# Unnormalized queries and keys in the gated delta rule of a hybrid block: the query scale in the output norm, the key scales in the rows of the triangular system

## The chip, the cores and the metric

One NeuronCore of a Trainium2 chip runs the whole block; nothing is shared with other cores. The time is the device time of one execution in microseconds. It was taken three times for the kernel before, and once more with the hardware profiler. TensorE multiplies matrices, VectorE, ScalarE and GpSimd work on tiles, and SyncE issues most loads.

## The reference, cut to what matters

The block reads 512 rows of width 2048 and sums three branches. The change is in the first one, a gated delta rule with 8 heads of width 128:

```python
qkv = jax.nn.silu(causal_depthwise_conv(qkv_raw, conv_w))
q = l2norm(q) * (GDN_HEAD_DIM ** -0.5)      # l2norm(x) = x * rsqrt(sum(x * x) + EPS)
k = l2norm(k)
k_beta = k * beta[..., None]
lower = where(strict, einsum(k_beta, k) * decay, 0)
rhs = concatenate([v * beta, k_beta * exp(gc)])
sol = triangular_solve(eye + lower, rhs)    # u_val, w_dec
qk = einsum(q, k) * decay
...                                         # scan over chunks: v_new, o, state
o = rmsnorm(o, out_norm_g)                  # o * rsqrt(mean(o * o) + EPS) * g
```

`beta` is a sigmoid per row and head, `gc` a running sum of log decays, `decay` their exponentiated differences. The other branches are a diagonal state space layer (S5) and an attention to 256 memory rows; gates, a projection and a last norm follow.

## The kernel before, in words

The program has five phases: attention, a mixer phase for the delta rule and S5 (with the projections of x for them), the gated unit of S5, the three merges, and the output projection. Nearly all of TensorE's work is the projections. A weight block of 128 output columns (16 tiles of 128x128) is loaded by SyncE into `raw`, split by ScalarE into a high part (`split_hi`, L406) and by VectorE into a low part (`split_lo`, L413), and multiplied with the high and low part of the activations: three products of 512 columns per tile (`mm3`, L419 to L421). `raw`, `wh` and `wl` have two buffers each. ScalarE copies the finished block out of its PSUM bank (`tile_out`).

**The mixer phase is a pipeline of three stages, written out by hand for each engine.** In one round, stage a runs the six projection blocks of head i, stage j the first part of head i-1 (convolution, norms, the triangular system and its inverse by levels, S5), and stage l the second part of head i-2 (weights, new values, states, output, output norm). Rounds for heads 0, 7 and the last output are unrolled; the six in between are a loop whose semaphore targets lie in registers. Each engine has a function `mixer` whose lines are the order of its queue. TensorE's (L924 to L991) places one piece of j or l work between eighths of a block, each of six products.

The order around the change, per round:

- TensorE: `norm_keys` (L789: the sum of squared keys over the partitions, L793, and running sums of decays, L796) behind the sixth eighth of block 1; `norm_queries` (L798) behind the second eighth of block 2; then `keys` (transposes of `kc`, L812), `keys_keys` (L820), `values` (L806), `turn_lower` (transposes of `dl`, L835), `keys_queries` (L828), and the levels, of which `level_x` 1 (L847) is the first. `level_x` 1 waits for `du`, which VectorE writes at L1651. `output_norm` (L894) is the sum of squared outputs.
- ScalarE (L1291 to L1313): `activation_of` (silu and the squares of queries and keys, L1240 and L1243), a sine table for S5, `output_root`, `key_root` (L1245: the root of the key sums, then `er`, an exponential), a sine table (L1227 to L1230), the copy-out of block 1 (`kraw`), L406 for block 3, `query_root` (L1252), `decays` (exponentials of `du` and `dl`, L1259 and L1261), and so on. Square roots, exponentials and sines each need a table load, which the compiler inserts.
- VectorE (L1720 to L1741): `convolve` for queries, keys and values, L413, four S5 combinations and scans, `gated` (L1683: a reciprocal and two products, the last being L1690), `differences` (L1606), `normed_keys` (a 128x512 reciprocal, L1619, and a product, L1621), L413 for block 3, `normed_queries` (L1625, L1627), `keys` (L1640, L1641), `system` (L1646), `values` (L1631), S5 combinations, `first_level` (L1657 to L1663), `queries` (L1651), L413, `level_x` 1.
- GpSimd (L552 to L620): arguments of the sines (`farg`), `turn_back` for S5, the store of the head before, `masks` (three products over 128x512, L594, L597 and L599, behind `decays`), further arguments, `decayed_queries` (L604), `turn_back`. VectorE's `keys` waits for the third of the masks (`pm` 3), `system` for the second.

`hph` holds four values per row and chunk of one head: `beta` (0), the sum of decays (1), `beta` times its exponential (2), and the log decay (3). PSUM bank 2 holds the squared-query sums, then the turned values, then keys by queries; bank 6 the squared-key sums, the turned keys and the turned `dl`; bank 7 the decays, then keys by keys.

The waits that tie `keys` to the others:

```python
dve.wait_ge(k.ktr, count(j, 1, 1))      # keys turned, TensorE
dve.wait_ge(k.dec, count(j, 2, 2))      # decays, ScalarE
dve.wait_ge(k.pm, count(j, 3, 4))       # third mask, GpSimd
tt(k.kbg[:, :, :], chunked(ps[6][:, :]), rows(k.hph[:, 2, :]), ALU.mult)
```

Of the kernel before, what the change touches and what calls it, by code (L numbers as in the profile page):

```python
# [51 lines left out]
COLS = ["eps", "eps128", "quarter", "even", "odd", "neven", "nodd"]  # L52
# [9 lines left out]
def constants():  # L62
# [11 lines left out]
    for n, v in enumerate([EPS, P * EPS, np.pi / 2, g2 == 0, g2 == 1, -(g2 == 0).astype(float), -(g2 == 1).astype(float)]):  # L74
        c[:, C_COL + n] = v
# [34 lines left out]
def build(nc, x, mem, norm_g, w_in, conv_w, a_log, dt_bias, gdn_g, lam_re, lam_im, log_dt, b_re, b_im,  # L110
          c_re, c_im, s5_d, w_glu, mem_g, w_kv, w_a, w_b, w_c, w_out, final_g, consts, out):
    with ExitStack() as ctx:
# [71 lines left out]
        with ExitStack() as area:  # L184
# [110 lines left out]
        k.qk, k.vtr, k.vb_s, k.ktr, k.kb, k.kk = \  # L295
            sems("qk", "vtr", "vb_s", "ktr", "kb", "kk")
# [236 lines left out]
def pool_program(k, pool):  # L533
# [18 lines left out]
    def mixer(j, l):  # L552
# [132 lines left out]
def tensor_program(k, pe):  # L685
# [238 lines left out]
    def mixer(a, j, l):  # L924
# [161 lines left out]
def scalar_program(k, act):  # L1086
# [150 lines left out]
    def activation_of(j, n):  # L1237
        t, sq = ((k.qc, k.rq), (k.kc, k.rk), (k.vc, None))[n]
        act.wait_ge(k.conv, count(j, 4 * n + 4, 12))
        act.activation(t[:, :], t[:, :], ACT.Silu).then_inc(k.silu, 1)  # L1240
        if sq is not None:
            act.wait_ge(k.silu, count(j, n + 1, 3))
            act.activation(sq[:, :], t[:, :], ACT.Square).then_inc(k.sq, 1)  # L1243

    def key_root(j):  # L1245
# [45 lines left out]
    def mixer(a, j, l, gate=None):  # L1291
# [580 lines left out]
```

## Time and profile before

| | |
|---|---|
| median of three runs | 2503.39 us (2502.95 to 2505.22) |
| span of the profiled execution | 2498.6 us |
| time of the profiled execution outside its span | not given on its own; the median lies 4.8 us above the span |
| TensorE busy | 2334.3 us, 93% |
| VectorE busy | 1211.7 us, 48% |
| ScalarE busy | 734.8 us, 29% |
| GpSimd busy | 696.0 us, 28% |
| mixer phase | about 441 to 1620 us, most heads some 130 us apart |

The profile's timelines list instructions by engine with their start and length; an instruction that stood idle before it has the idle time and the engine and line that ended it in brackets. Operations on one engine overlap by some hundredths of a microsecond. The granted clock is TensorE's, as a share of 2.4 GHz: 1.00 is 2.4 GHz and 0.50 is 1.2 GHz. L numbers are lines of the kernel before.

### The profile page before, as it was taken

The numbers are of one execution on the slowest core, as the hardware profiler recorded it, in microseconds if no ns is written. First come the engines' busy times: TensorE is split into PE (matmuls) and PEld (weight loads), VectorE is DVE, ScalarE is ACT, GpSimd is POOL, SyncE is SP. The second block draws the span as 40 slices with busy tenths as digits, with TensorE's granted clock in tenths as the row PEclk, the third lists the DMA queues.
The fourth block names the chain that finished last, engine by engine and source line by source line (L and its number), as shares of the span: only waits on it lengthen the run. The fifth ranks groups of instructions, "written<-read, shape, count | busy, mean of one in ns | idle before, by whom it ended". The sixth has DMA issues, their size and how long they took to land.

```text
span 2498.6 us, 28934 instructions
## 1 busy us (share of the span) xinstructions
PE 2334.3 (93%) x10744; PEld 1841.5 (74%) x10744; DVE 1211.7 (48%) x1319; ACT 734.8 (29%) x831; POOL 696.0 (28%) x538
## 2 busy tenths in 40 slices
PE   4999989999999999999989899989999999999996
PEld 3888868676666666666767578878888888887885
DVE  4433322858676776767685842333322232334223
ACT  5433322414142424232333423321221221223221
POOL 0000000756656565758483820010000000000000
PEclk9999999899999999998989899999999999999998
DMA  4544423222121122222222135544533333333332
GB/s 163 137 118 124 121 84 94 67 55 62 51 65 48 50 52 59 57 59 57 59 57 63 51 85 152 158 150 140 166 101 99 87 100 102 89 96 118 118 131 88
DMA packets 367431, 232.96 MB, mean 93 GB/s; under 512 B 20538, under 2 KB 348419, under 8 KB 365827
## 3 DMA queue, kind: packets, MB, share of 16 engines
q1 hardware_dynamic: 355954, 193.21, 28.6%
q0 software_dynamic: 9104, 34.61, 3.9%
q10 hardware_dynamic: 2304, 4.20, 0.4%
q8 instruction: 48, 0.79, 0.1%
q14 instruction: 21, 0.16, 0.0%
HBM read 213.11 MB, written 18.87 MB: 93 GB/s over the span
## 4 chain that ended last, share of the span: by engine, by line
PE 72%; POOL 11%; DVE 6%; issue 4%; ACT 4%; DMA 1%; POOLq 0%; SPq 0%; DVEq 0%; ACTq 0%
PE bank L419 21%; PE bank L421 21%; PE bank L420 21%; POOL karg L571 2%; PE bank L847 1%; POOL farg L573 1%; PE bank L857 1%; POOL karg L567 1%; POOL farg L569 1%; ACT wh L406 1%; PE bank L856 1%; DVE wl L413 1%; POOL pt L585 1%; POOL dl L594 1%; POOL hr L587 1%
## 5 line engine op out<-in xcount | busy, mean ns | idle before, releaser
L413 DVE TENSOR_TENSOR wl<-raw,wh 128x2048 fp32r<-128x2048 f32 x176 | 413.9, 2352 | 729.9 <-ACT wh L406 729.9
L419 PE MATMUL bank<-uh,wh 128*128 128x512 f32 (+1 forms) x1808 | 757.1, 419 | 4.9 <-POOLq L362 4.6
L420 PE MATMUL bank<-ul,wh 128*128 128x512 f32 (+1 forms) x1808 | 715.9, 396 | 0.0
L421 PE MATMUL bank<-uh,wl 128*128 128x512 f32 x1792 | 711.4, 397 | 0.0
L406 ACT ACTIVATE wh<-raw 128x2048 fp32r<-128x2048 f32 x176 | 336.1, 1910 | 429.2 <-PE bank L421 399.7
L419 PEld LDWEIGHTS bank<-uh,wh 128*128 128x128 f32 (+1 forms) x1808 | 346.1, 191 | 135.3 <-issue 66.8
L421 PEld LDWEIGHTS bank<-uh,wl 128*128 128x128 f32 x1792 | 343.8, 192 | 77.2
L420 PEld LDWEIGHTS bank<-ul,wh 128*128 128x128 f32 (+1 forms) x1808 | 346.8, 192 | 72.8 <-issue 8.1
L419 PE MATMUL bank<-gh,wh 128*128 128x512 f32 x512 | 202.6, 396 | 8.3 <-DVE gl L1779 8.3
L421 PE MATMUL bank<-gh,wl 128*128 128x512 f32 x512 | 201.0, 393 | 0.0
L420 PE MATMUL bank<-gl,wh 128*128 128x512 f32 x512 | 200.3, 391 | 0.0
L672 POOL DMA_DIRECT2D fg<-in_final_g_dram x1 | 0.6, 558 | 520.2 <-DVEq L362 520.2
L419 PEld LDWEIGHTS bank<-gh,wh 128*128 128x128 f32 x512 | 96.8, 189 | 28.9 <-issue 8.7
L421 PEld LDWEIGHTS bank<-gh,wl 128*128 128x128 f32 x512 | 96.6, 189 | 22.5
L420 PEld LDWEIGHTS bank<-gl,wh 128*128 128x128 f32 x512 | 96.7, 189 | 21.0
L541 POOL DMA_DIRECT2D gated_c<-ox x8 | 4.5, 563 | 365.6 <-DVE ox L1480 365.1
L419 PE MATMUL bank<-wh,uh 128*128 128x512 f32 x256 | 100.2, 391 | 3.3 <-DVE ul L1829 3.3
L421 PE MATMUL bank<-wh,ul 128*128 128x512 f32 x256 | 100.3, 392 | 0.0
L420 PE MATMUL bank<-wl,uh 128*128 128x512 f32 x256 | 100.3, 392 | 0.0
L1382 ACT ACTIVATE gates<-bank 128x512 f32<-128x512 f32 x32 | 19.1, 598 | 273.1 <-PE bank L421 273.1
L847 PE MATMUL bank<-tl,lt 128*128 128x128 f32 x384 | 58.9, 303 | 41.4 <-DVE du L1651 39.8
L847 PEld LDWEIGHTS bank<-tl,lt 128*128 128x128 f32 x384 | 55.4, 213 | 50.0 <-issue 42.9
(308 smaller groups left out, 3218.7 us busy)
## 6 DMA issues: line engine op xcount, KB each, us to landing
raw<-in_w_in_dram SPq DMA_DIRECT2D x224, 512.0 KB, 4.9
raw<-in_w_kv_mem_dram SPq DMA_DIRECT2D x32, 512.0 KB, 5.1
raw<-in_w_out_dram SPq DMA_DIRECT2D x32, 512.0 KB, 4.4
raw<-in_s_w_glu_dram SPq DMA_DIRECT2D x16, 512.0 KB, 5.1
raw<-in_w_br_c_dram SPq DMA_DIRECT2D x16, 512.0 KB, 5.0
raw<-in_w_br_b_dram SPq DMA_DIRECT2D x16, 512.0 KB, 4.7
raw<-in_w_br_a_dram SPq DMA_DIRECT2D x16, 512.0 KB, 4.6
xs<-in_x_dram SPq DMA_DIRECT2D x4, 1024.0 KB, 8.4
```

Source lines behind the costliest of these rows:

```text
L406: act.activation(k.wh[slot][:, :], k.raw[slot][:, :], ACT.Copy).then_inc(k.w_hi, 1)
L413: dve.tensor_tensor(k.wl[slot][:, :], k.raw[slot][:, :], k.wh[slot][:, :].bitcast(F32), ALU.subtract).then_inc(k.w_lo, 1)
L419: pe.matmul(o, ah, bh, start=start, stop=False)
L420: pe.matmul(o, ah, bl, start=False, stop=False)
L421: return pe.matmul(o, al, bh, start=False, stop=stop)
L567: ts(k.karg[:, :], k.karg[:, :], -ROUND, None, ALU.add).then_inc(k.args, 1)
L569: tt(k.farg[:, :], k.farg[:, :], k.karg[:, :], ALU.subtract).then_inc(k.args, 1)
L571: ts(k.karg[:, :], k.tvec, lo_, None, ALU.mult).then_inc(k.args, 1)
L573: tt(k.farg[:, :], k.farg[:, :], k.karg[:, :], ALU.add).then_inc(k.args, 1)
L585: pool.tensor_tensor(k.pt[:, :], c2[:, :], b[:, :], ALU.mult).then_inc(k.dem, 1)
L587: pool.tensor_tensor(o[:, :], o[:, :], k.pt[:, :], op).then_inc(k.dem, 1)
L847: mm = pe.matmul(ps[2][:, n * P:(n + 1) * P], k.lt[:, n, :], k.tl[:, n, :], start=True, stop=True)
```

## The change

The keys and queries are no longer divided by their norms. With s the inverse of the squared key norm of a row (plus epsilon), the triangular system becomes one for scaled unknowns: its row factor is `beta` times s instead of `beta`, `kbg` takes s as well, and the values take `beta` times the root of s. The sum of squared keys is taken with the rows on partitions, four narrow products into a 128x4 piece of bank 6, and VectorE works on 128x4 pieces (`hk`) where it worked on 128x512. The query norm is left to the output norm: the squared queries, times epsilon and constants, are added to the squared outputs in one PSUM group.

- Removed: `norm_queries` (TensorE), `query_root` (ScalarE), `normed_keys` and `normed_queries` (VectorE), the semaphore `qk`.
- Added: `key_scales` (VectorE, four 128x4 operations, in front of `differences`), one 128x4 product in `values`, a second product in `output_norm`, a 128x4 root in `key_root`.
- Moved: the squares (`key_squares` before the values' silu, `query_squares` behind `output_root`); `key_root` behind `row_decays` (the exponential `er`); it waits for `rn` 2, VectorE's reciprocal.
- New waits: GpSimd's second mask for `rn` 4, TensorE's `keys` for `rn` 1, VectorE's `convolve` for `sq` of the head before.

```diff
 # GpSimd, masks and decayed_queries
             wait_apart(k, pool, k.pm, count(j, 1, 4))
+            wait_apart(k, pool, k.rn, count(j, 4, 4))
             pool.tensor_tensor(k.dl[:, :, :], k.dl[:, :, :],
-                               k.hph[:, 0, :].unsqueeze(2).to_broadcast([P, NT, P]), ALU.mult).then_inc(k.pm, 1)
+                               k.hk[:, 2, :].unsqueeze(2).to_broadcast([P, NT, P]), ALU.mult).then_inc(k.pm, 1)
...
-            wait_apart(k, pool, k.qk, count(j, 2, 2))
+            wait_apart(k, pool, k.silu, count(j, 1, 3))
+            wait_apart(k, pool, k.er_s, count(j, 1, 1))
 # TensorE
-        pe.wait_ge(k.sq, count(j, 2, 2))
+        pe.wait_ge(k.sq, count(j, 1, 2))
         wait(pe, k.oroot, count(j, 0, 1))
-        pe.matmul(ps[6][:, :], ones, k.rk[:, :], start=True, stop=True).then_inc(k.ss, 1)
+        for n in range(NT):
+            mm = pe.matmul(ps[6][:, n:n + 1], k.rk[:, n * P:(n + 1) * P], ones[:, 0:1], start=True, stop=True)
+        mm.then_inc(k.ss, 1)
...
-    def norm_queries(j):
-        wait(pe, k.og, count(j, 0, 2))
-        pe.matmul(ps[2][:, :], ones, k.rq[:, :], start=True, stop=True).then_inc(k.ss, 1)
     def values(j):
         pe.wait_ge(k.silu, count(j, 3, 3))
-        pe.wait_ge(k.root, count(j, 2, 2))
+        wait(pe, k.og, count(j, 0, 2))
...
     def keys(j):
-        pe.wait_ge(k.qk, count(j, 1, 2))
+        pe.wait_ge(k.silu, count(j, 2, 3))
+        pe.wait_ge(k.rn, count(j, 1, 4))
...
     def keys_queries(j):
-        pe.wait_ge(k.qk, count(j, 2, 2))
+        pe.wait_ge(k.silu, count(j, 1, 3))
...
     def output_norm(j):
         pe.wait_ge(k.osq, count(j, 1, 1))
-        pe.matmul(ps[6][:, :], ones, k.lt[:, :, :], start=True, stop=True).then_inc(k.sso, 1)
+        pe.wait_ge(k.sq, count(j, 2, 2))
+        pe.matmul(ps[6][:, :], ones, k.lt[:, :, :], start=True, stop=False)
+        pe.matmul(ps[6][:, :], ones, k.rq[:, :], start=False, stop=True).then_inc(k.sso, 1)
 # ScalarE
+    def key_squares(j):
+        act.wait_ge(k.silu, count(j, 2, 3))
+        wait(act, k.ss, count(j, 0, 1))
+        act.activation(k.rk[:, :], k.kc[:, :], ACT.Square).then_inc(k.sq, 1)
+    def query_squares(j):
+        act.wait_ge(k.silu, count(j, 1, 3))
+        wait(act, k.sso, count(j, 0, 1))
+        act.activation(k.rq[:, :], k.qc[:, :], ACT.Square, scale=P * EPS ** 0.5).then_inc(k.sq, 1)
...
     def key_root(j):
-        act.wait_ge(k.ss, count(j, 1, 2))
-        act.activation(k.rk[:, :], ps[6][:, :], ACT.Sqrt, bias=col["eps"]).then_inc(k.root, 1)
+        act.wait_ge(k.rn, count(j, 2, 4))
+        act.activation(k.hk[:, 3, :], k.hk[:, 0, :], ACT.Sqrt).then_inc(k.root, 1)
...
-        if j: s5_matrices(j); activation_of(j, 1); activation_of(j, 2); s5_tables(j, 0)
+        if j: s5_matrices(j); activation_of(j, 1); key_squares(j); activation_of(j, 2); s5_tables(j, 0)
         if l: output_root(l)
-        if j: key_root(j); s5_tables(j, 1)
+        if j: query_squares(j); row_decays(j); key_root(j); s5_tables(j, 1)
         if a: out(1); split(2)
-        if j: query_root(j); decays(j); keep_z(j)
+        if j: decays(j); keep_z(j)
 # VectorE
+    def key_scales(j):
+        dve.wait_ge(k.ss, count(j, 1, 1))
+        ts(k.hk[:, 0, :], ps[6][:, 0:NT], EPS, None, ALU.add).then_inc(k.rn, 1)
+        dve.wait_ge(k.rn, count(j, 1, 4))
+        dve.reciprocal(k.hk[:, 0, :], k.hk[:, 0, :]).then_inc(k.rn, 1)
+        dve.wait_ge(k.rn, count(j, 2, 4))
+        tt(k.hk[:, 1, :], k.hk[:, 0, :], k.hph[:, 2, :], ALU.mult).then_inc(k.rn, 1)
+        tt(k.hk[:, 2, :], k.hk[:, 0, :], k.hph[:, 0, :], ALU.mult).then_inc(k.rn, 1)
     def values(j):
+        dve.wait_ge(k.root, count(j, 1, 1))
+        tt(k.hk[:, 3, :], k.hk[:, 3, :], k.hph[:, 0, :], ALU.mult).then_inc(k.kscale, 1)
         dve.wait_ge(k.vtr, count(j, 1, 1))
-        tt(k.vb[:, :, :], chunked(ps[2][:, :]), rows(k.hph[:, 0, :]), ALU.mult).then_inc(k.vb_s, 1)
+        dve.wait_ge(k.kscale, count(j, 1, 1))
+        tt(k.vb[:, :, :], chunked(ps[2][:, :]), rows(k.hk[:, 3, :]), ALU.mult).then_inc(k.vb_s, 1)
...
         wait(dve, k.vtr, count(j, 0, 1))
+        wait(dve, k.sq, count(j, 0, 2))
...
-        if j: differences(j); normed_keys(j)
+        if j: key_scales(j); differences(j)
         if a: split(2)
-        if j: normed_queries(j); keys(j); system(j); values(j); s5_states(j, 1, 0); s5_states(j, 1, 1)
+        if j: keys(j); system(j); values(j); s5_states(j, 1, 0); s5_states(j, 1, 1)
```

## Rows read from the trace of the kernel before

**Rows 1.** The page, section 2: TensorE's busy tenths in 40 equal slices of the span.

```profile
PE   4999989999999999999989899989999999999996
```

**Rows 2.** The windows of one head: start:end, length, busy us (instructions) of TensorE matmuls, weight loads, VectorE, ScalarE, GpSimd; granted clock; DMA share; GB/s.

```profile
981.50:1111.50 130.00, 118.49 (x538) 86.89 (x538) 92.33 (x108) 41.48 (x52) 83.17 (x60) 0.93 0.21 56
```

**Rows 3.** TensorE's timeline: start, us, engine, line, operation, count, in brackets idle before.

```profile
892.72 1.98 PE L847 MATMUL bank<-tl,lt 128*128 128x128 f32 x8 [5.00 <-DVE du L1651]
...
982.31 1.10 PE L793 MATMUL bank<-rk,cst 128*128 128x512 f32 x2 [0.91 <-ACT lt L1288]
983.24 1.02 PE L796 MATMUL bank<-gx,cst 128*128 128x512 f32 x2
...
993.49 2.07 PE L800 MATMUL bank<-rq,cst 128*128 128x512 f32 x2 [3.75 <-DVE kbg L1690]
...
1022.47 2.02 PE L847 MATMUL bank<-tl,lt 128*128 128x128 f32 x8 [4.97 <-DVE du L1651]
```

**Rows 4.** VectorE's timeline in the same head.

```profile
992.40 1.03 DVE L1690 TENSOR_TENSOR kbg<-kbg,zk 128x512 f32<-128x512 f32 x1
...
996.23 3.34 DVE L1619 RECIPROCAL rk<-rk 128x512 f32<-128x512 f32 x1
999.60 0.69 DVE L1621 TENSOR_TENSOR kc<-kc,rk 128x512 f32<-128x512 f32 x1
1000.21 2.28 DVE L413 TENSOR_TENSOR wl<-raw,wh 128x2048 fp32r<-128x2048 f32 x1
1002.41 3.35 DVE L1625 RECIPROCAL rq<-rq 128x512 f32<-128x512 f32 x1
1005.79 0.82 DVE L1627 TENSOR_TENSOR qc<-qc,rq 128x512 f32<-128x512 f32 x1
1006.54 0.68 DVE L1640 TENSOR_TENSOR kbg<-bank,hph 128x512 f32<-128x512 f32 x1
...
1021.64 0.68 DVE L1651 TENSOR_TENSOR du<-bank,du 128x512 f32<-128x512 f32 x1
```

**Rows 5.** ScalarE's timeline in the same head.

```profile
990.60 1.28 ACT L1227 ACT_TABLE_LOAD   x1 [4.56 <-POOL farg L575]
...
996.10 1.28 ACT L1255 ACT_TABLE_LOAD   x1
...
998.10 1.28 ACT L1259 ACT_TABLE_LOAD   x1
...
999.93 0.61 ACT L1261 ACTIVATE dl<-dl 128x512 f32<-128x512 f32 x1
```

**Rows 6.** GpSimd's timeline in the same head.

```profile
1000.73 2.88 POOL L594 TENSOR_TENSOR dl<-dl,cst 128x512 f32<-128x512 f32 x1 [0.38 <-ACT dl L1261]
...
1004.79 1.28 POOL L599 TENSOR_TENSOR du<-du,cst 128x512 f32<-128x512 f32 x1
```

**Rows 7.** Single lines of the program: count, then nanoseconds minimum/median/maximum, first and last start.

```profile
L594 POOL TENSOR_TENSOR dl<-dl,cst x8: 1268/2880/2888, 483.4 to 1390.9; 128x512 f32<-128x512 f32 x8
...
L1405 ACT ACTIVATE stat<-stat,cst x1: 298/298/298, 2480.9 to 2480.9; 128x4 f32<-128x4 f32 x1
...
L1432 DVE RECIPROCAL stat<-stat x2: 165/172/178, 22.6 to 28.2; 128x4 f32<-128x4 f32 x1, 128x2 f32<-128x2 f32 x1
```

**Rows 8.** Timelines of heads 0 (VectorE) and 7 (GpSimd), which stand outside the loop.

```profile
487.44 0.69 DVE L1640 TENSOR_TENSOR kbg<-bank,hph 128x512 f32<-128x512 f32 x1 [2.27 <-POOL du L599]
...
503.69 0.68 DVE L1651 TENSOR_TENSOR du<-bank,du 128x512 f32<-128x512 f32 x1
...
1390.90 2.39 POOL L594 TENSOR_TENSOR dl<-dl,cst 128x512 f32<-128x512 f32 x1 [1.50 <-ACT dl L1261]
```

**Rows 9.** Windows around the clock's return in two heads, and head 7's restart.

```profile
1032.00:1033.00 1.00, 1.00 (x4) 0.77 (x4) 0.00 (x0) 0.00 (x0) 1.00 (x2) 0.63 0.00 0
...
1413.14 2.05 PE L847 MATMUL bank<-tl,lt 128*128 128x128 f32 x8 [6.00 <-DVE du L1651]
...
1421.50:1422.00 0.50, 0.50 (x3) 0.40 (x2) 0.00 (x0) 0.00 (x0) 0.50 (x2) 0.64 0.00 0
```

More of the change, by code:

```diff
@@ L51 @@
 C_COL = C_T + S
-COLS = ["eps", "eps128", "quarter", "even", "odd", "neven", "nodd"]
+COLS = ["eps", "epssq", "quarter", "even", "odd", "neven", "nodd"]
 NCONST = C_COL + len(COLS)
@@ L73, in constants @@
     g2 = np.arange(P) // GS % 2
-    for n, v in enumerate([EPS, P * EPS, np.pi / 2, g2 == 0, g2 == 1, -(g2 == 0).astype(float), -(g2 == 1).astype(float)]):
+    for n, v in enumerate([EPS, P * EPS * EPS, np.pi / 2, g2 == 0, g2 == 1, -(g2 == 0).astype(float), -(g2 == 1).astype(float)]):
         c[:, C_COL + n] = v
@@ L209, in build @@
             k.hph = sb(area, "hph", [4, NT])
+            k.hk = sb(area, "hk", [4, NT])
             k.s5h = sb(area, "s5h", [5, 4])
@@ L294, in build @@
             sems("rsum", "root", "er_s", "dd", "dec", "rn")
-        k.qk, k.vtr, k.vb_s, k.ktr, k.kb, k.kk = \
-            sems("qk", "vtr", "vb_s", "ktr", "kb", "kk")
+        k.kscale, k.vtr, k.vb_s, k.ktr, k.kb, k.kk = \
+            sems("kscale", "vtr", "vb_s", "ktr", "kb", "kk")
         k.kq, k.pm, k.lm, k.qkt, k.ltr, k.lt_s = \
@@ L953, in mixer @@
         if a: big(a, 1, 6, 7); big(a, 2, 0, 1)
-        if j: norm_queries(j)
         if a: big(a, 2, 2, 3)
@@ L1237, in activation_of, with row_decays, key_root @@
     def activation_of(j, n):
-        t, sq = ((k.qc, k.rq), (k.kc, k.rk), (k.vc, None))[n]
+        t = (k.qc, k.kc, k.vc)[n]
         act.wait_ge(k.conv, count(j, 4 * n + 4, 12))
         act.activation(t[:, :], t[:, :], ACT.Silu).then_inc(k.silu, 1)
[L1241 to L1245, printed above, removed]
-        act.wait_ge(k.ss, count(j, 1, 2))
-        act.activation(k.rk[:, :], ps[6][:, :], ACT.Sqrt, bias=col["eps"]).then_inc(k.root, 1)
+    def key_squares(j):
[6 more added lines that the diff above has]
+        act.activation(k.rq[:, :], k.qc[:, :], ACT.Square, scale=P * EPS ** 0.5).then_inc(k.sq, 1)
+    def row_decays(j):
         act.wait_ge(k.rsum, count(j, 1, 1))
         act.activation(k.er[:, :, :], ps[7][:, :].rearrange("p (n c) -> p n c", n=NT), ACT.Exp).then_inc(k.er_s, 1)
-    def query_root(j):
-        act.wait_ge(k.ss, count(j, 2, 2))
-        act.activation(k.rq[:, :], ps[2][:, :], ACT.Sqrt, bias=col["eps128"], scale=float(P)).then_inc(k.root, 1)
+    def key_root(j):
+        act.wait_ge(k.rn, count(j, 2, 4))
+        act.activation(k.hk[:, 3, :], k.hk[:, 0, :], ACT.Sqrt).then_inc(k.root, 1)
     def decays(j):
@@ L1287, in output_root @@
         act.wait_ge(k.sso, count(l, 1, 1))
-        act.activation(k.lt[:, :, :], ps[6][:, :].rearrange("p (n c) -> p n c", n=NT), ACT.Sqrt, bias=col["eps"],
+        act.activation(k.lt[:, :, :], ps[6][:, :].rearrange("p (n c) -> p n c", n=NT), ACT.Sqrt, bias=col["epssq"],
                        scale=1 / P).then_inc(k.oroot, 1)
@@ L1615, in differences @@
         ts(k.dl[:, :, :], k.dl[:, :, :], 0.0, None, ALU.max).then_inc(k.dd, 1)
-    def normed_keys(j):
-        dve.wait_ge(k.root, count(j, 1, 2))
-        dve.reciprocal(k.rk[:, :], k.rk[:, :]).then_inc(k.rn, 1)
-        dve.wait_ge(k.rn, count(j, 1, 2))
-        tt(k.kc[:, :], k.kc[:, :], k.rk[:, :], ALU.mult).then_inc(k.qk, 1)
-    def normed_queries(j):
-        dve.wait_ge(k.root, count(j, 2, 2))
-        dve.reciprocal(k.rq[:, :], k.rq[:, :]).then_inc(k.rn, 1)
-        dve.wait_ge(k.rn, count(j, 2, 2))
-        tt(k.qc[:, :], k.qc[:, :], k.rq[:, :], ALU.mult).then_inc(k.qk, 1)
+    def key_scales(j):
[6 more added lines that the diff above has]
+        tt(k.hk[:, 2, :], k.hk[:, 0, :], k.hph[:, 0, :], ALU.mult).then_inc(k.rn, 1)
     def values(j):
+        dve.wait_ge(k.root, count(j, 1, 1))
+        tt(k.hk[:, 3, :], k.hk[:, 3, :], k.hph[:, 0, :], ALU.mult).then_inc(k.kscale, 1)
         dve.wait_ge(k.vtr, count(j, 1, 1))
-        tt(k.vb[:, :, :], chunked(ps[2][:, :]), rows(k.hph[:, 0, :]), ALU.mult).then_inc(k.vb_s, 1)
+        dve.wait_ge(k.kscale, count(j, 1, 1))
+        tt(k.vb[:, :, :], chunked(ps[2][:, :]), rows(k.hk[:, 3, :]), ALU.mult).then_inc(k.vb_s, 1)
     def keys(j):
@@ L1639, in keys @@
         wait(dve, k.g_st, count(j, 0, 16))
-        tt(k.kbg[:, :, :], chunked(ps[6][:, :]), rows(k.hph[:, 2, :]), ALU.mult).then_inc(k.kb, 1)
+        dve.wait_ge(k.rn, count(j, 3, 4))
+        tt(k.kbg[:, :, :], chunked(ps[6][:, :]), rows(k.hk[:, 1, :]), ALU.mult).then_inc(k.kb, 1)
         tt(k.kd[:, :, :], chunked(ps[6][:, :]), k.du[:, :, P - 1:P].to_broadcast([P, NT, P]), ALU.mult).then_inc(k.kb, 1)
```

## Prediction

> **What bounds the kernel now.** I read the page first. TensorE's slices are nearly all nines [rows 1], so a change pays only where TensorE waits or runs at its lower clock. Then the windows cut per head: in the mixer stage TensorE is busy 118.5 of 130 us and its mean granted clock is 0.93 [rows 2]; a head takes 129.7 us, from the restart at L847 at 892.72 to the next at 1022.47 [rows 3]. So about 11.5 us of a head are idle and some 9 us of clock (0.07 x 130) are lost. Its timeline says where: 4.97 us before L847 on VectorE's `du` (L1651), 3.75 us before L800 on `kbg` (L1690), 0.91 us before L793 on ScalarE's `lt` [rows 3]. The change touches the first two.
>
> Which of them sets a head's end? After the wait at L800, TensorE runs some 24 us of work and then stops again at L847 until 1022.47 [rows 3]. Whatever it gains before 1017.5 it waits away at L847. So L847's release decides, and that is VectorE's L1651. VectorE is busy without a gap from 980.5 to 1022.3; the stretch from L1690 to L1651 is shown in [rows 4]. At first sight 8 us leave just this chain. So I followed the two engines that feed it: ScalarE, whose `dl` exponential (L1261) ends at 1000.54 [rows 5], and GpSimd, whose masks start 0.2 us later and end at 1006.07 [rows 6]. VectorE's `keys` (L1640) waits for the third mask and starts at 1006.54. So the GpSimd chain is only 0.47 us short of being the bound today.
>
> **The change part by part, in the head that starts at 981.5.**
>
> VectorE loses L1619 (3.34 us), L1621 (0.69), L1625 (3.35) and L1627 (0.82): 8.2 us [rows 4]. It gains five operations of 128x4; one costs about 0.2 us with its wait, by the 128x4 reciprocal of 178 ns [rows 7]. Four of them stand behind `gated`, so `differences` ends near 997 and VectorE then waits for the split of block 3 (L413, behind ScalarE's L406).
>
> ScalarE loses `query_root` (a table load and the root, from 996.10 to the next load at 998.10 [rows 5]) from in front of the exponentials: 2.0 us. The two squares stay, moved; the query one stands behind `output_root`, where ScalarE next waits for TensorE or GpSimd. But `key_root` now needs `rn` 2, two small VectorE operations behind L1690, and that ends at 992.40 + 1.03 = 993.43 [rows 4]. Small operations 0.4 and 0.1 of signalling give 993.9. Then a load of 1.28 and a 128x4 root of 0.30 [rows 7] end at 995.5. Everything ScalarE did from the load at 990.60 to the one at 996.10 (sine table, `kraw`, L406) stands behind it: 5.5 us, to 1001.0. The exponential table, `du` and `dl` took 998.10 to 1000.54, 2.44 us: they end at 1003.5, that is **2.9 us later** than before. What is queued behind the new wait is thus all of ScalarE's work up to L1261, and GpSimd waits for that. The loads of the loop start only after the wait in front of them: the one at 990.60 came after 4.56 us of idling [rows 5], so I don't let the root's load hide. The second sine table, `kraw` and block 3's high half come 4.9 us later too, and L413 behind it frees `raw` for SP's next load 0.9 us later; their users on VectorE and TensorE stand behind 1008, and SP's load of about 5 us has until ScalarE's next L406 at 1013, so I put these at nothing.
>
> GpSimd starts L594 at 1003.6 instead of 1000.73. It took 2.88 us there, since it began while VectorE's L413 ran (1000.21 to 1002.49); the fastest of the eight took 1.27 [rows 4, 6, 7]. Now L413 runs from 1001.05 to 1003.35, just ahead of it, and VectorE then idles: I take 1.27. That returns 1.6 us, and the third mask is done 1.3 us later, at 1007.4. `keys` starts 0.1 behind it: 1007.5 against 1006.54, +0.95. The scale in `values` adds 0.2 and the extra waits of `convolve` 0.05. L1651 and with it L847 come **1.2 us later**. L594 at its old 2.88 is the upper end for this step (+2.8); full cover by the 0.47 us of today and no signalling is the lower one (+0.8).
>
> TensorE: `norm_queries` goes (two passes of 512 columns, 0.93 us by L793's at full clock [rows 3]), and its wait; eight narrow products replace L793's two, bounded between nothing and 1.9, twice what L793 takes; I take the same 0.93. New waits at `keys` (`rn` 1, 993.6), `keys_keys` and, above all, `turn_lower`: it needs L1646, now near 1009, while TensorE arrives near 1004.5. None of this counts, for TensorE still reaches L847 before 1020, even with 5 us at the lower clock; the cover is the wait at L847, which grows to 5 us or more. `output_norm` gains one product, 0.93 us. In a head it fits the 0.9 us before L793 [rows 3], where otherwise it would cost 0.9. In the last round there is no such wait: it is paid once.
>
> VectorE from L1640 to L1651 took 15.1 us with GpSimd working beside it [rows 4]; in head 0 the same stretch took 16.3 (487.44 to 503.69 [rows 8]). How the two engines meet changes a little, so between -1 and +1.1 us a head; I take nothing, as the two start as far apart as before (2.7 against 2.8 us).
>
> The lower clock: it comes back 10.3 us after the restart at 1022.47 (the row from 1032 is low for 0.74 us), but 8.7 us after the one at 1413.14 [rows 3, 9]. A us at 1.2 GHz instead of 2.4 costs half a us of work: 4.4 to 5.1 us a head. New restarts will fall elsewhere in this span; I take back 0.3 a head, bounds -0.8 and +0.8.
>
> Six heads in the loop: 6 x (1.2 - 0.3) = 5.4. Head 0 has no `gated`, and its `keys` already waited 2.27 us for the mask [rows 8], which waits for GpSimd's own queue: +0.2. Head 7's loads are 1.28 us for each gate output too; there L594 took 2.39 [rows 8] and gives back only 1.1 of 2.9, less the cover of 0.4, plus the scale: +1.6. Last round +0.9. **Sum +8.1 us.** The profiled span of 2498.6 becomes 2506.7; the median of the runs lies 4.8 above that span, and gives 2511.5.
>
> A page speaks against more: the Trainium skill, "ScalarE: Activation LUTs", section "What ACT_TABLE_LOAD costs", puts a drain of 1.38 us behind each load, 2.66 us in all. By that the three loads behind `rn` 2 would make L1651 4.1 us later still, and the kernel some 33 us slower than my sum; the rows show 1.28 us and a function 0.01 us behind it (998.10 + 1.28, `dl` done by 1000.54) [rows 5], so this rival has a chance below 0.01.
>
> **The rivals.**
> (a) The delay is returned by the clock, or GpSimd has less to wait: L1651 comes 0.8 us later or less, and the clock, coming back at an unchanged moment after a later restart, gives most of it back. Then only the last round and head 7 remain: +2 to +3, about 2506. For it: head 7's late restart lost less [rows 9]. Chance 0.3.
> (b) Faster: ScalarE's root isn't held by `gated`. The place is `key_root`'s wait; the point is whether `rn` 2 is there before GpSimd has computed `farg` (990.4). Then `dl` ends 2 us earlier, L594 starts unblocked near 1000.7 and takes 1.27, and `keys` starts near 1004.6: -1.9 + 0.2, some -1.7 us for seven heads, with the last round about -11: 2492. Against it: two VectorE operations and 3.3 us of reciprocal stand in front of `rn` 2 in program order. Chance 0.12.
> (c) L594 still collides with L413 (the margin is 0.3 us), or the stretch to L1651 takes head 0's 16.3 us: 1.1 to 1.6 us more in six heads, 2518 to 2521. Chance 0.12.
> (d) The saved VectorE time reaches L847 whole (8 heads x 7 us, 2447): it would need `keys` to start near 1000, before GpSimd has masks to give. 0.01.
> My forecast has 0.45, and its far lower tail (VectorE and GpSimd meeting better by 1 us a head) reaches below 2498 with 0.01.
>
> **How the numbers follow.** 0.2% is 5 us, about what a measurement of this kernel can tell. Forecast and (c) are slower by more, and a tenth of (a) too; the forecast's lower tail falls within 5 us. Slower 0.55, same 0.31, faster 0.14. The range from 2498 to 2518 leaves out (b), (d) and half of (c), 0.19 in all.
>
> **What the new profile would show.** `key_root`'s load starting near 994 after a wait for VectorE; L1261 ending near 1003.5 on this head's clock; L594 at 1.3 us; VectorE idle near 997 to 1001 and 1003.3 to 1007.5, the second on GpSimd's `du`; TensorE waiting about 5 us before the transposes of `dl` and over 5 before the first level; none before the keys but 1 to 2 us; a head of about 130.6 us. Wrong if `keys` isn't waiting for GpSimd, if the exponentials end before 1001, or if a head is under 129.7 us.

## The result, and the profile after

The changed kernel took **2522.98 us** in the median of 4 runs (2521.75 to 2524.17), the kernel before 2504.3 in 4 runs beside it (2502.95 to 2505.92): a ratio of 1.0078, 95% interval 1.0064 to 1.0092. It is slower by 19 us. The forecast was 2511.5, slower, with a range to 2518: the direction was right, the size less than half of what came, and the time is outside the range. The profiled execution has a span of 2520.6 us, 22.0 above the one before: TensorE's idle time grew by 13.6 us (164.3 to 177.9) and its busy time by 8.4.

The page of the changed kernel, busy time and the slices of TensorE and its clock:

```profile
PE 2342.7 (93%) x10792; PEld 1848.0 (73%) x10792; DVE 1169.3 (46%) x1327; ACT 723.5 (29%) x822; POOL 679.1 (27%) x538
...
PE   4999989899898989898989799999999999999996
...
PEclk9999999999898989898979899999999999999998
```

VectorE's four instructions did go (its busy time falls from 1211.7 to 1169.3 us), yet TensorE's slices show more eights in the mixer stage than [rows 1]. Who makes TensorE wait there? The waits of the changed kernel's TensorE from 441 to 1650 us (engine, tile and line, releaser; us in total, times, longest):

```profile
PE bank L849 <- DVE du L1663: 68.6, 8, 9.7
PE bank L814 <- DVE hk L1630: 7.8, 7, 1.5
PE bank L822 <- DVE dl L1622: 7.6, 7, 1.1
```

and the same of the kernel before, from 441 to 1620 us:

```profile
PE bank L847 <- DVE du L1651: 39.8, 8, 6.0
PE bank L800 <- DVE kbg L1690: 25.7, 7, 3.8
PE bank L812 <- DVE kc L1621: 8.7, 8, 4.0
```

The 34 us of waits for `kbg` and `kc` have become 15, and the wait for `du` has grown from 39.8 to 68.6. So the new time is in VectorE's chain to `du`. The head that answers to [rows 4 to 6] has its `gated` at 1003.61, where the old one had 992.40. ScalarE's timeline in it:

```profile
996.05 1.28 ACT L1264 ACT_TABLE_LOAD   x1
1005.00 0.20 ACT L1264 ACTIVATE hk<-hk 128x4 f32<-128x4 f32 x1 [7.67 <-DVE hk L1632]
1005.22 1.28 ACT L1230 ACT_TABLE_LOAD   x1
...
1012.55 0.61 ACT L1270 ACTIVATE dl<-dl 128x512 f32<-128x512 f32 x1
```

VectorE and GpSimd in the same head, in one timeline (L1702 is the old L1690, L595 the old L594, L1652 the old L1640, L1721 the old L1709, L570 the old L569, L1725 the old L1713, L1669 the old L1657, L1663 the old L1651). Two instructions in it matter most: `gr`, VectorE's product for the S5 scans, and `farg`, GpSimd's product for the arguments of the sines; both have two inputs in SBUF:

```profile
1003.61 1.08 DVE L1702 TENSOR_TENSOR kbg<-kbg,zk 128x512 f32<-128x512 f32 x1
...
1010.74 2.29 DVE L414 TENSOR_TENSOR wl<-raw,wh 128x2048 fp32r<-128x2048 f32 x1 [1.79 <-ACT wh L407]
...
1013.36 1.28 POOL L595 TENSOR_TENSOR dl<-dl,cst 128x512 f32<-128x512 f32 x1 [1.79 <-ACT dl L1270]
...
1017.20 0.69 DVE L1652 TENSOR_TENSOR kbg<-bank,hk 128x512 f32<-128x512 f32 x1 [4.17 <-POOL du L601]
...
1019.01 0.15 DVE L1639 TENSOR_TENSOR hk<-hk,hph 128x4 f32<-128x4 f32 x1
1019.26 0.69 DVE L1642 TENSOR_TENSOR vb<-bank,hk 128x512 f32<-128x512 f32 x1
...
1021.17 1.29 POOL L570 TENSOR_TENSOR farg<-farg,karg 128x512 f32<-128x512 f32 x1 [0.18 <-POOL karg L568]
1021.18 1.82 DVE L1721 TENSOR_TENSOR gr<-ma,mb 128x512 f32<-128x512 f32 x1
...
1025.09 2.19 DVE L1725 TENSOR_TENSOR_SCAN gr<-s5h,gr 128x512 f32<-128x512 f32 x1
1027.21 1.56 DVE L1725 TENSOR_TENSOR_SCAN gi<-s5h,gi 128x512 f32<-128x512 f32 x1
1028.69 1.69 DVE L1669 TENSOR_TENSOR tl<-dl,cst 128x512 f32<-128x512 f32 x1
...
1035.32 0.68 DVE L1663 TENSOR_TENSOR du<-bank,du 128x512 f32<-128x512 f32 x1
```

and the lines of the kernel before that stand between the L1640 and L1651 of [rows 4]:

```profile
1010.24 0.69 DVE L1709 TENSOR_TENSOR gr<-ma,mb 128x512 f32<-128x512 f32 x1
1010.39 1.71 POOL L569 TENSOR_TENSOR farg<-farg,karg 128x512 f32<-128x512 f32 x1 [0.18 <-POOL karg L567]
...
1013.02 1.59 DVE L1713 TENSOR_TENSOR_SCAN gr<-s5h,gr 128x512 f32<-128x512 f32 x1
1014.53 1.19 DVE L1713 TENSOR_TENSOR_SCAN gi<-s5h,gi 128x512 f32<-128x512 f32 x1
1015.65 1.71 DVE L1657 TENSOR_TENSOR tl<-dl,cst 128x512 f32<-128x512 f32 x1
```

Counted from the end of `gated` (993.43 before, 1004.69 after):

| from the end of `gated`, in the head read | before | after |
|---|---|---|
| `dl` exponential ends | 7.1 | 8.5 |
| third mask ends | 12.6 | 12.5 |
| `keys` starts | 13.1 | 12.5 |
| `keys` to the first level (L1657, L1669) | 9.1 | 11.5 |
| `keys` to `du` (L1651, L1663) | 15.1 | 18.1 |

`keys` starts 0.6 us earlier, yet `du` comes 2.4 later: the stretch from `keys` to `du` takes **3.0 us longer**. The timelines say where. The scale product puts `vb` 0.25 later (the pitch from `dl` to `vb` was 0.60 and is 0.85). The product `gr` started 0.15 us ahead of GpSimd's `farg` before and took 0.69, while `farg` took 1.71. Now it starts 0.01 us behind `farg` and takes 1.82, while `farg` takes 1.29: its pitch to the next instruction is 1.13 longer. The scans give up another 0.97 (2.63 from the first one to the first level before, 3.60 now), and the four products from there to `du` 0.64. Together 2.99.

A theory comes from that: two products of inputs in SBUF, one on each engine, don't run side by side, and the one that starts first goes through. (The pair at 1021.17 lasts 1.83 us from its first start to its last end, where 0.69 and 1.29 in turn would be 1.98.) The change moved the phase of the two queues by a hair. Against GpSimd's instruction behind the masks (1006.17, L564, before; 1017.27, L565, after) `keys` started 0.37 us late and now starts 0.07 early: VectorE gained 0.44. From `keys` to `gr` it is 3.70 us before and 3.98 after (the scale product): 0.28 lost. And GpSimd reaches `farg` 4.22 us behind that instruction before, 3.90 after: 0.32 lost. So a lead of 0.15 became a lag of 0.01. The rivals: the 3 us are the scale product and its waits themselves, or they come from the later exponentials.

### The profile page after: what moved, and what is told of

It reads as the page before. It is cut to its first block, busy times and chain, and to the rows that moved or that the text cites. A ratio compares the mean times of both kernels' runs of the same rounds, so it can differ in the third digit from the quotient of the medians.

```text
span 2520.6 us, 29089 instructions
## 1 busy us (share of the span) xinstructions
PE 2342.7 (93%) x10792; PEld 1848.0 (73%) x10792; DVE 1169.3 (46%) x1327; ACT 723.5 (29%) x822; POOL 679.1 (27%) x538
## 4 chain that ended last, share of the span: by engine, by line
PE 77%; DVE 11%; issue 4%; ACT 3%; POOL 2%; DMA 1%; DVEq 0%; SPq 0%; POOLq 0%; ACTq 0%
PE bank L420 22%; PE bank L422 22%; PE bank L421 21%; PE bank L849 2%; PE bank L859 2%; PE bank L858 1%; PE bank L918 1%; PE bank L925 1%; DVE gi L1725 1%; PE bank L926 1%; PE bank L919 1%; DVE tl L1697 1%; DVE mb L1719 1%; DVE gr L1721 1%; PE bank L754 1%
## 5 line engine op out<-in xcount | busy, mean ns | idle before, releaser
L849 PE MATMUL bank<-tl,lt 128*128 128x128 f32 x384 | 59.1, 303 | 68.6 <-DVE du L1663 68.6
```

What stands on the lines that cost most here:

```text
L849: mm = pe.matmul(ps[2][:, n * P:(n + 1) * P], k.lt[:, n, :], k.tl[:, n, :], start=True, stop=True)
```

## The experiments

Runs 1 to 4 stood beside a kernel before of 2502.47 us (23 runs), runs 5 to 8 beside 2501.92 (7 runs), run 9 beside 2501.7 (7 runs). Ratios are against these.

**1. The scale product in front of `keys`.** The same work, but done in VectorE's idle time.

```
+    def value_scale(j):                       # its wait and its product, out of values
...
-        if j: keys(j); system(j); values(j); ...
+        if j: value_scale(j); keys(j); system(j); values(j); ...
```

> The changed kernel with one line moved: VectorE makes the 128x4 scale of the values in front of keys, where it stands idle, and no longer between system and values. In the changed kernel the stretch from the start of kbg to the start of du takes 18.1 us a head against 15.1 before, and the first S5 difference gr in it starts 0.01 us behind GpSimd's farg product and takes 1.82 us instead of 0.69. Theory A (the two engines exclude each other, and who starts first decides): VectorE is now 0.25 us earlier and comes first, so the stretch falls by 2 to 3 us to 15 to 16, and the kernel to 2500 to 2509 us. Theory B (the stretch grew by the work and the waits put into it): it falls by the 0.25 us that left it, the kernel to about 2521.

2505.69 us (2503.31 to 2507.08, 10 runs), ratio 1.0013 [1.0003, 1.0022]: of the 18.7 us over the kernel before, 3.2 are left. In the timeline `gr` is ahead again, by 0.25 us:

```profile
1011.05 0.69 DVE L1723 TENSOR_TENSOR gr<-ma,mb 128x512 f32<-128x512 f32 x1
1011.30 1.59 POOL L570 TENSOR_TENSOR farg<-farg,karg 128x512 f32<-128x512 f32 x1 [0.18 <-POOL karg L568]
```

`keys` starts 12.5 us behind `gated`, as in the change, and the stretch to `du` is back at 15.1 in each of the six heads of the loop. In head 0 and head 7 `farg` stays ahead of `gr`, and their stretches stay at 17.8 and 17.7. So the later exponentials aren't the cause. Whether the product's own duration is, or its phase, the next run asks.

**2. The kernel before, with a useless product of 128x4.** It stands where the change has its scale product, with a wait on it.

```
+        tt(k.pad[:, :], k.hph[:, 0, :], k.hph[:, 1, :], ALU.mult).then_inc(k.kscale, 1)
         dve.wait_ge(k.vtr, count(j, 1, 1))
+        dve.wait_ge(k.kscale, count(j, 1, 1))
```

> The kernel before, with a 128x4 product that nobody needs between system and values on VectorE, and a wait for it, as the change has one there. Nothing else differs. There the first S5 difference gr starts 0.15 us ahead of GpSimd's farg product. Theory A: 0.25 us more puts it behind, so the stretch from kbg to du grows from 15.1 to 17 to 18.1 us, and the kernel takes 2515 to 2527 us. Theory B: 0.25 us a head, about 2506.

2521.64 us (2520.95 to 2522.65, 4 runs), ratio 1.0078 [1.0061, 1.0094]: **one instruction of 0.15 us, put into the kernel before, makes it as slow as the change does.** The stretch is 18.0 us in every head of the loop, `keys` stands at 13.1 as before, and `gr` is now 0.12 us behind `farg`:

```profile
1019.32 0.15 DVE L1632 TENSOR_TENSOR pad<-hph 128x4 f32<-128x4 f32 x1
...
1021.37 1.29 POOL L571 TENSOR_TENSOR farg<-farg,karg 128x512 f32<-128x512 f32 x1 [0.18 <-POOL karg L569]
1021.49 1.72 DVE L1713 TENSOR_TENSOR gr<-ma,mb 128x512 f32<-128x512 f32 x1
```

**3. The change, with GpSimd held back instead.** A memset of 32 unread columns stands between the masks and GpSimd's next arguments (the edit is written on one line here); VectorE's work is untouched, the scale product still in its place.

```
-        if j: masks(); arguments(2); ...
+        if j: masks(); pool.memset(k.pad[:, :], 0.0); arguments(2); ...
```

> The changed kernel with one more instruction on GpSimd, a memset of 32 columns of a tile nobody reads, behind the masks and in front of the next arguments. Theory A: GpSimd's farg product now starts later by the length of that instruction and VectorE's gr comes first, so the stretch from kbg to du falls to 15 to 16.5 us, and the kernel gets faster by work that was added: 2500 to 2512. Theory B: no change or slightly slower, 2523 to 2525.

2505.37 us (2503.6 to 2506.93, 10 runs), ratio 1.0011 [1.0001, 1.0021]. An instruction **added** to the other engine gives some 16 us back (2.9 us over the kernel before are left of 18.7). The stretch is 15.4 in five heads of the loop and 14.2 in one; the lead is 0.03 us, and 0.04 in the one:

```profile
1006.99 0.12 POOL L626 MEMSET pad<- 128x32 f32 x1
...
1011.06 0.69 DVE L1725 TENSOR_TENSOR gr<-ma,mb 128x512 f32<-128x512 f32 x1
1011.09 1.83 POOL L571 TENSOR_TENSOR farg<-farg,karg 128x512 f32<-128x512 f32 x1 [0.18 <-POOL karg L569]
```

With runs 1 and 2 this leaves the order of the two starts as the cause of the 3 us: work was moved, added on VectorE and added on GpSimd, and each time the stretch and the kernel followed the order. The order doesn't set the whole length. With `gr` ahead by 0.03 to 0.04 us the stretch was 15.4 and 14.2 here, and 16.2 to 16.3 in heads 0 and 7 of the kernel before: the pairs further on meet in their own ways.

**4. The root taken from the sums directly.** ScalarE takes the root of the sums in PSUM, with the small constant as its bias, right behind `output_root`, so that it doesn't stand behind `gated`; VectorE inverts the root and squares it.

```
-        act.wait_ge(k.rn, count(j, 2, 4))
-        act.activation(k.hk[:, 3, :], k.hk[:, 0, :], ACT.Sqrt).then_inc(k.root, 1)
+        act.wait_ge(k.ss, count(j, 1, 1))
+        act.activation(k.hk[:, 3, :], ps[6][:, 0:NT], ACT.Sqrt, bias=col["eps"]).then_inc(k.root, 1)
...
-        if j: query_squares(j); row_decays(j); key_root(j); s5_tables(j, 1)
+        if j: key_root(j); query_squares(j); row_decays(j); s5_tables(j, 1)
...
```

> The changed kernel, but ScalarE takes the root of the key sums straight from PSUM, behind output_root, and VectorE takes the reciprocal of the root and squares it. ScalarE then waits for nothing on VectorE in front of the exponentials. The first exponentials dl should end 5.1 us behind the end of gated instead of 8.5 (2.0 less than the 7.1 before), and GpSimd's masks start behind its store, some 7.5 us behind gated. If the held root was what made the change slow (theory C), keys starts 1 to 1.5 us earlier and the kernel gains 8 to 12 us, to 2511 to 2515. By theory A the gain depends on how VectorE and GpSimd meet in the stretch behind it, which starts with both at the same distance: it stays near 18 us and the kernel near 2511 to 2518 too, still slower than before; what tells them apart is the length of the stretch, 15 by C alone, 18 by A.

2509.07 us (2507.53 to 2510.7, 8 runs), ratio 1.0028 [1.0017, 1.0039]. The exponentials end 5.1 us behind `gated` in place of 8.5, but of these 3.4 us `keys` gets only 1.2 (11.3 in place of 12.5): the first mask takes 1.80, and the masks now wait for GpSimd's own earlier work (the first starts 0.03 us behind the store of the head before). The stretch remains 18.1 in five heads. In the head at 1000 us the two products start at the same moment, VectorE has the better of it, the stretch is 15.4 and the head 127.5 us, where the others take 130.4 to 131.7. Without that head the time would be some 3 us higher by estimate, and inside the expected range, which it misses by 2 us:

```profile
1015.54 0.69 DVE L1721 TENSOR_TENSOR gr<-ma,mb 128x512 f32<-128x512 f32 x1
1015.54 1.85 POOL L570 TENSOR_TENSOR farg<-farg,karg 128x512 f32<-128x512 f32 x1 [0.18 <-POOL karg L568]
...
1144.32 1.28 POOL L570 TENSOR_TENSOR farg<-farg,karg 128x512 f32<-128x512 f32 x1 [0.18 <-POOL karg L568]
1144.33 1.82 DVE L1721 TENSOR_TENSOR gr<-ma,mb 128x512 f32<-128x512 f32 x1
```

One kernel, two heads, 0.01 us apart: the nearest thing to a direct look at the tie. The root's place is a second, smaller cost of the change.

**5. VectorE's idle time filled.** The change frees VectorE and then lets it wait 4.2 us for GpSimd's mask, with 8.8 us of S5 products and scans queued behind (1019.87 to 1028.69). Here that work comes first.

```
-        if j: keys(j); system(j); values(j); s5_states(j, 1, 0); s5_states(j, 1, 1)
+        if j: s5_states(j, 1, 0); s5_states(j, 1, 1); keys(j); system(j); values(j)
```

> The changed kernel with VectorE's order changed alone: the S5 combinations and scans of the second quarter stand in front of keys instead of behind system and values. In the changed kernel VectorE idles 4.2 us before keys, for GpSimd's mask, and 1.8 before L414. If the saved VectorE time was only turned into this waiting (theory D), the 7 us of S5 work now fill it: du is written some 6 us earlier behind gated (24 to 25 us instead of 30.6), TensorE's own work becomes the bound before L849, and the kernel takes 2473 to 2490 us, faster than before the change. If what bounds the head lies elsewhere (TensorE's work and clock), it stays within 5 us of 2523.

**2439.14 us** (2438.47 to 2442.97, 4 runs), ratio 0.9753 [0.9737, 0.977]: 63 us below the kernel before, and so some 82 below the change, which stood 19 above it; it gained more than was expected. Of the 83.4 us between the two profiled spans, 52.6 are idle time of TensorE and 30.9 are busy time for the same 10792 instructions: less of them fall into stretches at 1.2 GHz (99.6 us of busy time there, 163.1 in the change). In the head read, VectorE goes from its low part of block 3 to `du` with no more than 0.43 us of idle time, right in front of `du`. Three of the four products of the first level take 0.68 to 0.70 us where they took 1.69 to 1.75, as the two engines' products meet otherwise; the fourth, behind a `farg`, still takes 1.78:

```profile
975.47 1.64 DVE L1725 TENSOR_TENSOR_SCAN gi<-s5h,gi 128x512 f32<-128x512 f32 x1
977.03 0.66 DVE L1652 TENSOR_TENSOR kbg<-bank,hk 128x512 f32<-128x512 f32 x1
...
980.59 0.70 DVE L1669 TENSOR_TENSOR tl<-dl,cst 128x512 f32<-128x512 f32 x1
...
982.42 1.78 DVE L1675 TENSOR_TENSOR tu<-cst,tu 128x512 f32<-128x512 f32 x1
984.63 0.69 DVE L1663 TENSOR_TENSOR du<-bank,du 128x512 f32<-128x512 f32 x1 [0.43 <-PE bank L830]
```

From `gated` (ended 960.7) to `du` it is 23.9 us, where it was 28.2 before and 30.6 in the change. TensorE no longer waits for `du` at all; the largest wait left in the mixer stage is at the transposes of `dl`, 21.2 us over 8 heads.

**6. Runs 5, 1 and 4 together.**

> As the run with the S5 work in front of keys, and with the two other edits: the root of the key sums straight from PSUM, and the values' scale made before keys. ScalarE's exponentials end 3.4 us earlier, but the masks are now needed only 14 us behind gated and are there after 11.3, so the earlier root should be worth 1 us a head or less where TensorE's second S5 input holds VectorE: 2468 to 2488 us.

**2433.04 us** (2431.86 to 2435.49, 4 runs), ratio 0.9723 [0.9707, 0.9739]: the best version of the study, 6 us below run 5. The gain over run 5 is within what was expected (1 us a head or less); the time lies below the expected range because run 5's did.

**7. The query half of the change alone,** on the kernel before: the query scale moved into the output norm, `norm_queries`, `query_root` and `normed_queries` gone, the keys normalized as before.

```
-        if j: norm_queries(j)
...
-        if j: query_root(j); decays(j); keep_z(j)
+        if j: decays(j); keep_z(j)
...
-        if j: normed_queries(j); keys(j); ...
+        if j: keys(j); ...
```

> The kernel before with the query half of the change alone: no query norm, its squares added in the output norm; the keys are normalized as before. Theory A: keys starts 12.3 to 12.7 us behind gated (GpSimd's mask, 13.1 before), there is no scale product in the stretch behind it, VectorE comes first and the stretch stays 15.1 us: 2499 to 2505 us, no change that a measurement shows, though 4.2 us a head of VectorE and 2.0 of ScalarE are gone. Theory B (the cost goes with the parts): half of the 20 us, about 2512.

2513.16 us (2511.22 to 2514.61, 4 runs), ratio 1.0042 [1.0025, 1.0059]. A miss: it was to be the cheap half, and is 11 us slower than the kernel before, more than half of the loss. The number is the second theory's (about 2512), but the reason is another one. VectorE stops in front of `vb`, for values that TensorE hasn't turned yet, since TensorE now stands in front of the keys:

```profile
1006.98 0.69 DVE L1623 TENSOR_TENSOR kc<-kc,rk 128x512 f32<-128x512 f32 x1
...
1007.73 1.11 PE L809 MATMUL bank<-cst,kc 128*128 128x128 f32 x4 [7.92 <-DVE kc L1623]
...
1018.00 0.69 DVE L1627 TENSOR_TENSOR vb<-bank,hph 128x512 f32<-128x512 f32 x1 [2.78 <-PE bank L803]
```

Before, TensorE waited 3.75 us a head at L800, in `norm_queries`, and 0.55 for `kc`; with the first gone, it runs ahead into the wait for `kc` (7.9 us), and what is queued behind `kc` comes late. Much of it comes late by the clock: of the 14.4 us that the span is longer than before, 9.8 are busy time of TensorE for the same 10744 instructions. The whole change doesn't have this wait, as its keys need no `kc` from VectorE. So the two halves' losses can't be added up to the whole: this one's wait disappears with the other half. The other half alone was not run.

**8. Run 6 with TensorE's next input products in front of the wait.** `s5_inputs(j, 1)` stands where `norm_queries` was.

```
+        if j: s5_inputs(j, 1)
         if a: big(a, 2, 2, 3)
-        if j: keys(j); keys_keys(j); s5_inputs(j, 1)
+        if j: keys(j); keys_keys(j)
```

> As the one with the three edits, and TensorE multiplies the inputs of the second S5 quarter where norm_queries stood, so that VectorE can start this quarter as soon as its low part of block 3 is done, 5 us behind gated. Then keys follows near 12 us behind gated with the masks just there, and du near 21 instead of 30.6. TensorE, with no wait left before L849 but the ones for dl turned, should set the end: a head of 123 to 126 us and 2455 to 2475 us. If VectorE was not what held TensorE, nothing is gained over the run without this edit.

2445.78 us (2442.12 to 2448.92, 4 runs), ratio 0.977 [0.9754, 0.9787]. Also a miss: below the expected range, but 13 us slower than run 6, which it was to improve on. TensorE's waits in front of the keys are filled (7.9 us in run 6, none here), but VectorE had no idle time there that earlier inputs could have filled: `keys` stands 16.2 us behind `gated` in both runs. So TensorE only arrives earlier at the transposes of `dl` and waits there:

```profile
PE bank L837 <- DVE dl L1661: 56.2, 8, 7.7
```

against 20.7 in run 6. In all, TensorE's idle time is 26.8 us longer than in run 6 and its busy time 13.4 us shorter.

**9. The reorder of run 5 on the kernel before.** How much of the 63 us has the change any part in?

```
-        if j: normed_queries(j); keys(j); system(j); values(j); s5_states(j, 1, 0); s5_states(j, 1, 1)
+        if j: normed_queries(j); s5_states(j, 1, 0); s5_states(j, 1, 1); keys(j); system(j); values(j)
```

> The kernel before, with the same reorder of VectorE's work as the one that gave 2439.1 on the changed kernel: the two scans' steps 1,0 and 1,1 stand in front of keys, system and values. Theory (the reorder pays because the change freed 8.2 us of VectorE's chain, which then only waited for GpSimd's mask): before has no such wait (keys starts 0.47 us behind the mask with VectorE busy), so the two states (about 9 us with their scans) come in front of the chain that TensorE waits for and push L1651 later by what they take, less what no longer stands beside GpSimd: TensorE already waits there 5 us, so the head gets up to 4 to 7 us longer until the scans' work, which otherwise stood behind, closes the gap; 2515 to 2560. Rival (the reorder pays by itself, because it takes the scans out of GpSimd's way, whatever the change): 2440 to 2480, and then the change has no part in the 62 us.

2471.93 us (2470.12 to 2473.43, 4 runs), ratio 0.9882 [0.9865, 0.9898]. **My theory was wrong here, and the rival's number nearer:** the reorder pays 30 us even where VectorE has no idle time to fill. Its waits of TensorE from 441 to 1620 us:

```profile
PE bank L835 <- DVE dl L1646: 39.8, 8, 5.6
PE bank L800 <- DVE kbg L1690: 25.8, 7, 3.8
PE bank L812 <- DVE kc L1621: 8.2, 8, 4.1
```

In sum TensorE waits as long as before, 39.8 us over 8 heads (5.6 a head in the loop, where it was 5.0); the wait has moved from the first level to the transposes of `dl`. What changed is the clock behind it. Windows of the kernel before, behind the restart at 1022.47 (the clock is the third number from the end):

```profile
1024.00:1026.00 2.00, 2.00 (x5) 1.02 (x4) 1.59 (x2) 0.00 (x0) 2.00 (x1) 0.50 0.00 0
...
1030.00:1032.00 2.00, 2.00 (x6) 1.61 (x5) 0.79 (x1) 0.00 (x0) 1.64 (x3) 0.50 0.05 12
```

and of this run, behind its restart at 998.94:

```profile
1000.00:1002.00 2.00, 2.00 (x7) 1.56 (x6) 2.00 (x2) 0.60 (x1) 2.00 (x2) 0.53 0.00 0
1002.00:1004.00 2.00, 2.00 (x13) 1.69 (x11) 2.00 (x2) 1.63 (x2) 1.82 (x3) 1.00 0.00 0
```

The first is at 1.2 GHz for 10.3 us behind the restart, the second is back at 2.4 GHz 3 us behind it. What that is worth stands in TensorE's busy time. For the same 10744 instructions it falls from 2334.3 to 2306.1 us, 28.2 of the 30.3 us by which the span is shorter; its idle time falls by 2.1. In the stretches at 1.2 GHz, summed over the trace, TensorE is busy for 143.8 us before and 87.9 here, and half of the difference is 27.9. The rival's own reason, that the scans get out of GpSimd's way, is not what pays: VectorE's busy time falls by only 3.4 us (1211.7 to 1208.3), and `du` comes 29.8 us behind `gated`, 1.6 later than before.

With that the four corners are known:

| | scans behind `values` | scans in front of `keys` |
|---|---|---|
| before | 2502 | 2471.9 |
| changed | 2523 | 2439.1 |

The change costs 19 us in the one order (against the 2504.3 beside it) and brings 33 in the other. Its saved VectorE time is real, but in the old order it ends in VectorE's wait for the masks.

## Why the prediction was wrong in size

Step by step, by its own headings.

- **What bounds a head.** Right: TensorE's first level waits for VectorE's `du`, all through. The wait grew, from 5.0 to between 8.0 and 9.7 us a head.
- **ScalarE.** Wrong by half. It said that "the loads of the loop start only after the wait in front of them" and added the root's load of 1.28 us to the chain. The load stands at 996.05, in front of the wait of 7.67 us, and costs nothing; the exponentials end 1.4 us later, not 2.9. The load of [rows 5] at 990.60, from which I argued, does come after its wait, but the trace of before also had the other case, in head 7 and at the same line: there the load runs ahead of the wait. I took one pattern for a rule; what decides between the two, no run here separates.

```profile
1376.26 1.28 ACT L1227 ACT_TABLE_LOAD   x1
1380.16 0.63 ACT L1227 ACTIVATE tsin<-farg 128x512 f32<-128x512 f32 x1 [2.62 <-POOL farg L575]
```

- **GpSimd.** L594 falls from 2.88 to 1.28 us, and it starts just behind L413: as stated. The cover of 0.47 us is used up: as stated. With ScalarE's error, `keys` comes 0.6 us earlier instead of 0.95 later. `keys` waits for GpSimd (4.17 us), as stated.
- **TensorE.** Right that what happens before the first level is covered by the wait there. The forecast wait of 5 us at the transposes of `dl` didn't come in the loop; it came once, in head 7 (4.6 us).
- **The stretch from `keys` to `du`: this is the step that failed.** The prediction took nothing, with bounds of -1 and +1.1 us, "as the two start as far apart as before (2.7 against 2.8 us)". It measured **+3.0 us in all six heads of the loop** (18.1 against 15.1), +1.6 in head 0 and +1.5 in head 7. The prediction doesn't say between which instructions these 2.7 and 2.8 us lie, and no row shows them. Its own terms held a shift: `keys` 0.47 us behind the third mask before and 0.1 in the forecast, and 0.2 more for the scale product. What decides is which of `gr` and `farg` starts first, and there the lead was 0.15 us, which the prediction doesn't have: [rows 4, 6] leave out the lines between. The bound from head 0 (16.3) was another case: there `gr` is 0.03 us ahead of `farg` and takes 0.69 (491.15), and the 1.1 us more come from pairs further on (the second product takes 1.13 where it takes 0.69 in the loop, the second scan 2.26 where it takes 1.19). So it bounded nothing of what a lost lead costs. Runs 1 to 3 show the cause.
- **The clock.** I took back 0.3 us a head. None came back: the clock returns 10.5 us behind the restart in the mean of the loop heads, against 10.3 before. Within the bounds stated, and small; yet runs 5, 7 and 9 show that large sums lie there. I priced the length of a wait and left its place alone, and in run 9 some 28 us hang on the place.
- **Head 0, head 7, last round.** Head 0 +0.2 predicted, +1.95 measured at its restart (`keys` +0.4, stretch +1.6). Head 7 +1.6 predicted, +2.5 measured: its `keys` is 1.5 later, as reckoned, and its stretch adds 1.5 which wasn't reckoned (the time before its `gated` gives 0.5 back). The 1.5 at `keys` came out by luck: the root's load is hidden there too (1392.93, the root at 1400.78), and in its place the sine table's load, which ran ahead before (1376.26), now stands behind the root (1401.00). The rest of the kernel +1.6, with +0.9 predicted.

The sum by the restarts of the first level: before at 504.51, 633.34, 762.98, 892.72, 1022.47, 1152.17, 1281.93 and 1413.14; after at 506.46, 638.21, 770.55, 903.26, 1036.14, 1167.56, 1299.78 and 1433.51. Six loop heads add 15.9 us, where 5.4 was predicted; 2.4 a head is -0.6 and +3.0. The other 0.25 a head lies between the restart and the end of the next `gated`, and goes with the clock: where it comes back 11.6 us behind the restart (903.26), 0.7 us is lost there, and where it comes back after 8.4 (1036.14), 0.7 is gained.

Rival (c) named the right place, but with a price of 1.1 to 1.6 us a head and a chance of 0.12. Two errors of opposite sign, 1.5 us too much at `keys` and 3.0 too little behind it, made the forecast look nearer than its reasoning was. The Trainium skill, "SBUF — State Buffer", section "Who interferes with whom", says that a VectorE instruction with two inputs in SBUF contends with a GpSimd instruction that reads SBUF, that the ports they share are an exclusive lock, and that the order of issue decides who blocks. The traces agree: 0.69 against 1.82 us for `gr`, 1.28 against 2.88 for the first mask, and either engine can be the one that loses. Had I laid the two queues side by side by that rule, with starts to 0.01 us, the lead of 0.15 us would have stood out, and a range of ±1 could not have stood.

## What to carry to other kernels

Where two engines shut one another out, the order of their starts is a cost term by itself: look for pairs that start within some 0.3 us of one another (an added 0.27 turned this one, from 0.15 ahead to 0.12 behind), price both orders, and take the difference as the bound, since any small edit can turn it. When an edit frees an engine that then waits for another, ask at once which queued work could fill the wait: here one line of order was worth more than the change, and turned its sign. And waits of the same sum cost 28 us more or less here according to where they stood, by the clock behind them, so sum waits and low clock by place before calling one of them the bound.

## What the runs showed of the hardware

- A tie of 0.01 us between `gr` and `farg` is worth 2.75 us in the stretch (15.37 against 18.12 in two heads of run 4). One more instruction of 0.15 us, which turned a lead of 0.15 us into a lag of 0.12, made the kernel 19 us slower (run 2).
- ScalarE's table load ran ahead of the wait of the function that it serves (996.05, then 7.67 us of waiting, then the root at 1005.00), and so was free; so did the one at 1376.26 in the kernel before, while the one at 990.60 came behind its wait of 4.56 us. The next function starts 0.02 us behind a load here (1005.22 + 1.28, `tsin` at 1006.52).
- A VectorE product of 128x4 is not always small: 0.15 us at 1005.75 and 1019.01, but 0.82 us at 1005.00 in the changed kernel and 1.06 at 978.81 in run 5, each time beside a product on GpSimd, and ending within 0.02 us of it.
- 39.8 us of waiting, in sum, in front of two different places of TensorE's program left the clock low for 10.3 us in the one and 3 in the other (run 9, the head read). What of the work behind the restart decides that, no run here separates.
